# Attention heads: f32 products of latents in three passes of rounded parts

## The chip, the cores and the metric

The kernel runs on one core of a Trainium2 chip. The metric is the device time of one execution in microseconds (us).

## The reference

The kernel computes two blocks in f32. The first mixes 512 tokens of 1024 channels with a gated spatial layer and a recurrence. The second has latent attention with 16 heads, then a state space mixer. The change lies in the attention, which is this:

```python
def block(args):
    qa, qr, cs, sn = args
    q_pos = jnp.concatenate([qa, _apply_rope(qr, cs[:, None], sn[:, None])], axis=-1)
    q_free = jnp.concatenate([qa, qr], axis=-1)
    s_all = jnp.concatenate([jnp.einsum('bthd,bkd->bhtk', q_pos, keys_lat),
                             jnp.einsum('bthd,bkd->bhtk', q_free, keys_ctx)], axis=-1)
    p = jax.nn.softmax(s_all.astype(jnp.float32) * scale, axis=-1).astype(ckv_l.dtype)
    return (jnp.einsum('bhtk,bkc->bthc', p[..., :s], ckv_l)
            + jnp.einsum('bhtk,bkc->bthc', p[..., s:], ckv_c))
```

`keys_lat` and `keys_ctx` are the 128 latent channels `ckv` with 64 rope channels `kr` behind them, for 512 tokens and for 256 tokens of context. The context's queries attend to the context alone.

## The kernel before

Each engine runs its own program in order, and semaphores (`at(step)`) join them. TensorE (PE) is written out by hand in `head_pe`, ScalarE (ACT) in `head_act`, VectorE (DVE) in `head_dve`. SyncE (SP) loads the weights in the order of one stream, each tile of 512 KB into one of 6 ring slots when the tile 6 places ahead of it has been used.

**Input projection** (`mla_in_pe`, `mla_in_act`, `mla_in_dve`): 20 weight tiles, each 8 steps of a 256- and a 512-column product in f32. ACT evacuates each tile. PE sums the latents' squares beside it and transposes the normalized latents behind tile 15; DVE copies them to `ckv_tm` (L2257). In between DVE makes 16 tiles of powers for the state space mixer (`c_pow_dve`, L2043 and L2045, 6 operations each), which GpSimd stores: tiles 0 to 5 first, 12 to 15 behind `ckv_tm`. GpSimd makes tables (`tables_pool`) once all 16 are stored.

**Heads** (`head_pe`): a head has six units n of 128 queries: two of the context with 256 keys, four with 768 keys. For each unit:
- *scores*: the queries `q_abs` by the latents `ckv` (L2306), then the rope part (L2317), into one of two pairs of PSUM banks; always two units together;
- *softmax*: DVE takes the maximum (L2426, L2428), ACT the exp (L2446), DVE normalizes (L2435, L2437);
- *transposes* (`turn`, L2331): 2 or 6 into PSUM banks 6 and 7, and ACT copies them to SBUF (`pt_act`, L2456 or L2461). The banks are there once, so the next unit's transposes wait for that copy.

For each head come the *values* (L2342, 2 context tiles and 6 latent tiles of 512 columns), their copy `o_lat` (L2515), the up-projection (L2349) and the gate product on DVE (L2533). The next head is prepared in three steps: *fold* (L2374), *abs* (L2378, makes `q_abs`, copied at L2474), *rope* (L2387, copied at L2477, turned on DVE at L2523 to L2528). PE's order in head h, with n its first unit: transposes n-2, scores n and n+1, fold h+1, transposes n-1, scores n+2 and n+3, values h-1, transposes n and n+1, scores n+4 and n+5 with the up-projection of h-1 inside, transposes n+2, abs h+1, transposes n+3, rope h+1.

An f32 matmul stands in the trace as two instructions, a matmul on values rounded to `fp32r` as one. The trace calls both f32. Other products of the kernel are already in three passes of rounded parts: x = high + low, and high x high + high x low + low x high is summed in PSUM (L470 and L2739, for instance).

**Output projection** (`mla_out_pe`, L2563): 8 tiles in f32; DVE adds the residual from `xT` and `ctxT` and makes 15 tiles of powers (`b_pow_dve`, L2170). It begins when all engines have ended the heads.

## Time and profile before

| what | us |
|---|---|
| median of 3 runs | 2201.29 |
| lowest, highest | 2197.02, 2205.79 |
| profiled execution, its time | 2202.79 |
| profiled execution, span | 2200.9 |
| PE busy | 2091.2 |
| DVE busy | 1241.8 |
| ACT busy | 768.8 |
| GpSimd busy | 626.4 |
| chain that ended last, share of PE | 88% |

The span is from the first to the last instruction. The time also has what lies around it. In the span the input projection runs from about 470 to 676 us, the heads from 676 to 1130 and the output projection from 1130 to 1296. Busy times of PE are modelled at the ends of matmuls, so starts are read from start to start.

### The profile page before, as it was taken

What the parts mean: (1) busy time and instruction counts of PE and PEld (TensorE: products, weight loads), DVE (VectorE), ACT (ScalarE), POOL (GpSimd) and SP (SyncE); (2) the same over time, 40 slices, a digit from 0 to 9 for tenths busy, and PEclk for the clock granted to TensorE, in tenths of its full rate; (3) what the DMA queues carried; (4) which work ended last, traced back from release to release, by engine and by line L of the source; (5) the groups of instructions that cost most, each with busy time, mean ns of one, the idle gap of its engine ahead of it and who ended that gap; (6) DMA issues with size and microseconds to landing.
All of it is one profiled execution on the core that took longest, in us unless ns stands there. A gap on an engine that the chain in (4) does not pass through costs nothing.

```text
span 2200.9 us, 38924 instructions
## 1 busy us (share of the span) xinstructions
PE 2091.2 (95%) x15596; PEld 1508.5 (69%) x15596; DVE 1241.8 (56%) x1897; ACT 768.8 (35%) x1425; POOL 626.4 (28%) x1129
## 2 busy tenths in 40 slices
PE   7999998999998999999989978999989999999996
PEld 6887787765554555555555647888867788888785
DVE  3367664459995444444448856888993233333344
ACT  3335543231103444444410026555544322232223
POOL 2543211410015888888811221111121000000000
PEclk9999999999999999999999999999999999999999
DMA  9221443422452111111126433999974222222221
GB/s 360 78 96 51 154 156 118 163 85 96 167 192 100 53 53 53 53 53 58 53 93 239 165 120 108 308 304 304 307 214 170 86 96 96 96 96 96 96 86 39
DMA packets 119411, 292.42 MB, mean 133 GB/s; under 512 B 11616, under 2 KB 57056, under 8 KB 113088
## 3 DMA queue, kind: packets, MB, share of 16 engines
q1 hardware_dynamic: 107072, 226.10, 30.9%
q0 software_dynamic: 12160, 63.84, 7.8%
q8 instruction: 124, 2.03, 0.4%
q14 instruction: 55, 0.45, 0.1%
HBM read 223.97 MB, written 65.93 MB: 132 GB/s over the span
## 4 chain that ended last, share of the span: by engine, by line
PE 88%; DVE 6%; ACT 2%; issue 2%; POOL 1%; DMA 0%; SPq 0%; DVEq 0%; ACTq 0%; POOLq 0%
PE psum L470 30%; PE psum L1867 8%; PE psum L2563 8%; PE psum L2739 6%; PE psum L2306 5%; PE psum L2342 5%; PE psum L2317 3%; PE psum L1142 3%; PE psum L2331 2%; PE psum L2387 2%; PE psum L2909 2%; PE psum L2378 2%; PE psum L304 2%; PE psum L2859 1%; PE psum L2968 1%
## 5 line engine op out<-in xcount | busy, mean ns | idle before, releaser
L470 PE MATMUL psum<-split,w_split 128*128 128x512 f32 x1632 | 371.5, 389 | 0.0
L470 PEld LDWEIGHTS psum<-split,w_split 128*128 128x128 f32 x1632 | 306.3, 188 | 63.8
L452 DVE TENSOR_TENSOR w_split<-ring,w_split 128x512 fp32r<-128x512 f32 x182 | 129.0, 709 | 308.7 <-ACT w_split L447 308.3
L2088 POOL TENSOR_TENSOR early<-early 128x8 f32<-128x8 f32 (+6 forms) x672 | 277.1, 412 | 52.8
L447 ACT ACTIVATE w_split<-ring 128x512 fp32r<-128x512 f32 x182 | 115.0, 632 | 335.3 <-PE psum L470 332.3
L1867 PE MATMUL psum<-early,ring 128*128 128x512 f32 (+1 forms) x544 | 176.3, 486 | 0.0
L2739 PE MATMUL psum<-h,u_w 128*128 128x256 f32 (+1 forms) x768 | 158.6, 352 | 14.8 <-ACT u_t L2651 11.4
L2563 PE MATMUL psum<-gate,ring 128*128 128x512 f32 (+1 forms) x512 | 165.4, 486 | 1.2 <-issue 1.2
L1867 PEld LDWEIGHTS psum<-early,ring 128*128 128x128 f32 x544 | 103.3, 190 | 71.2 <-issue 64.1
L2563 PEld LDWEIGHTS psum<-gate,ring 128*128 128x128 f32 x512 | 97.2, 190 | 69.3 <-issue 62.7
L2739 PEld LDWEIGHTS psum<-h,u_w 128*128 128x128 f32 x768 | 119.7, 193 | 34.6 <-issue 18.8
L470 PE MATMUL psum<-h,w_split 128*128 128x512 f32 x552 | 134.6, 404 | 7.9 <-DVE w_split L452 7.9
L470 PE MATMUL psum<-h_split,in_w 128*128 128x512 f32 x600 | 138.8, 391 | 0.5 <-POOL in_w L459 0.5
L459 POOL TENSOR_TENSOR u_w<-ring,u_w 128x512 fp32r<-128x512 f32 x42 | 54.0, 1285 | 276.1 <-ACT u_w L447 238.8
L470 PEld LDWEIGHTS psum<-h,w_split 128*128 128x128 f32 x552 | 106.3, 194 | 34.9 <-DVE w_split L452 5.4
L353 POOL TENSOR_TENSOR early<-xT 128x512 f32<-128x512 f32 x1 | 1.3, 1290 | 452.2 <-DVE xT L3287 452.2
L470 PEld LDWEIGHTS psum<-h_split,in_w 128*128 128x128 f32 x600 | 111.9, 188 | 25.9 <-ACT prev L806 0.8
L2306 PE MATMUL psum<-ckv,q_abs 128*128 128x256 f32 (+1 forms) x320 | 111.4, 480 | 8.2 <-ACT prob L2446 5.8
L2426 DVE TENSOR_REDUCE early<-psum 128x1 f32<-128x768 f32 (+1 forms) x96 | 74.9, 780 | 78.0 <-PE psum L2317 76.1
L2342 PE MATMUL psum<-area,ckv_tm 128*128 128x512 f32 (+1 forms) x256 | 102.5, 554 | 1.0 <-ACT area L2461 1.0
L459 POOL TENSOR_TENSOR in_w<-ring,in_w 128x512 fp32r<-128x512 f32 x50 | 77.3, 1545 | 78.0 <-ACT in_w L447 75.8
L2342 PEld LDWEIGHTS psum<-area,ckv_tm 128*128 128x128 f32 x256 | 48.4, 194 | 53.5 <-issue 50.3
(442 smaller groups left out, 3480.9 us busy)
## 6 DMA issues: line engine op xcount, KB each, us to landing
ring<-in_s_glu SPq DMA_DIRECT2D x64, 512.0 KB, 3.5
ring<-in_w_mod SPq DMA_DIRECT2D x48, 512.0 KB, 5.3
made_c_pow<-area POOLq DMA_DIRECT2D x16, 1152.0 KB, 4.8
c_pow<-made_c_pow SPq DMA_DIRECT2D x32, 576.0 KB, 5.2
ring<-in_s_in SPq DMA_DIRECT2D x32, 512.0 KB, 6.5
made_b_pow<-area POOLq DMA_DIRECT2D x15, 1024.0 KB, 4.5
b_pow<-made_b_pow SPq DMA_DIRECT2D x15, 1024.0 KB, 10.5
ring<-in_w_in SPq DMA_DIRECT2D x25, 512.0 KB, 3.5
```

Source lines behind the costliest of these rows:

```text
L447: nc.scalar.activation(rounded(buffer(u, 0)), source(u), ACT.Copy).then_inc(act_done, 1)
L452: nc.vector.tensor_tensor(rounded(buffer(u, 1)), source(u), buffer(u, 0), ALU.subtract).then_inc(dve_done, 1)
L459: nc.gpsimd.tensor_tensor(rounded(buffer(u, 1)), source(u), buffer(u, 0), ALU.subtract).then_inc(pool_done, 1)
L470: ins = nc.tensor.matmul(out, rounded(buffer(u, w)[:, ks]), values(x, k), start=(first and k == 0 and n == 0), stop=(last and k == UNIT_K ...
L1142: ins = nc.tensor.matmul(psum[half(odd), b, a + tt * CHUNK:a + (tt + 1) * CHUNK], lhs(half(odd), tt), rhs(half(odd), tt), start=True, stop ...
L1867: ins = nc.tensor.matmul(o, tile_w(("mla_in", m), k), h2[:, k, a:a + n], start=(k == 0), stop=(k == KD - 1))
L2088: nc.gpsimd.tensor_tensor(o, a, b, op).then_inc(pool_done, 1)
L2306: mm(o, q_abs_of(h, u), ckv[:, a:a + m], start=True, stop=False)
L2342: ins = mm(o, ckv_tm[:, k, :], pt[:, k, :], start=(k == 0), stop=(k == kt - 1))
L2426: v.tensor_reduce(sm[:, n % 3, 0:1], both(b)[:, 0:keys], AX.X, ALU.max).then_inc(dve_done, 1)
L2563: ins = nc.tensor.matmul(o, tile_w(("mla_out", 2 * m + k // KD), k % KD), gate2[:, k, a:a + n], start=(k == 0), stop=(k == KE - 1))
L2739: ins = nc.tensor.matmul(o, rounded(u_w[:, u % 4, w, kk * P:(kk + 1) * P]), h3_part(x, k)[:, a:a + size], start=(k == 0 and n == 0), stop= ...
```

## The change

The latent part of the scores and the latent part of the values go from f32 to three passes of rounded parts. The rope part, the context's values and all projections stay in f32.

- *Scores*: `q_abs` becomes `q_abs_high`, which ACT writes rounded in place of its plain copy, and `q_abs_low`, which DVE makes as PSUM minus high (two operations). `ckv` gets `ckv_high` (ACT, behind tile 14 of the input projection) and `ckv_low` (DVE).
- *Values*: for units 2 to 5 of a head ACT's copy of the transposes is rounded (`pt_high`), and DVE makes `pt_low_a` and `pt_low_b` as PSUM minus high (two operations a unit). `ckv_tm` gets `tm_high` (ACT, behind tile 18) and `tm_low` (DVE, right behind `ckv_tm`). The 6 transposes of a unit now lie in 768 adjacent columns, and fold uses the first 256 columns of bank 6.
- *Waits*: transposes wait for the low part of the unit before; rope waits for `q_abs_low`, fold for the low part of unit n-2, values for the last `pt_low`.
- *Memory*: `high` and `pt_low_a` lie where `xT` is, `pt_low_b` where `ctxT` is. So SP stores `xT` to HBM behind the first block (2 MB), and loads it and `ctxT` back (2 MB and 1 MB) when the last values are done. `mla_out_dve` waits for that.

```diff
+                if m == 14:
+                    act.wait_ge(x_kept, 16)
+                    act.wait_ge(*at("ckv_normed"))
+                    nc.scalar.activation(rounded(ckv_parts[0]), ckv[:, :], ACT.Copy).then_inc(act_done, 1)
+                    act.wait_ge(act_done, act_count.up("ckv_high"))
+                if m == 18:
+                    act.wait_ge(*at("ckv_tm"))
+                    nc.scalar.activation(rounded(high[:, 3, :]), ckv_tm[:, :, :].rearrange("p k c -> p (k c)"), ACT.Copy).then_inc(act_done, 1)
+                    act.wait_ge(act_done, act_count.up("tm_high"))
 
         def mla_in_dve(dve):
             v = nc.vector
...
+            dve.wait_ge(*at("tm_high"))
+            v.tensor_tensor(rounded(tm_low[:, :, :]), ckv_tm[:, :, :], tm_parts[0], ALU.subtract).then_inc(dve_done, 1)
+            dve.wait_ge(dve_done, dve_count.up("tm_low"))
+            v.tensor_tensor(rounded(ckv_parts[1][:, :]), ckv[:, :], ckv_parts[0], ALU.subtract).then_inc(dve_done, 1)
+            dve.wait_ge(dve_done, dve_count.up("ckv_low"))
             for m in range(12, KE):
                 c_pow_dve(dve, m)
...
                 pe.wait_ge(*at("q_abs", h))
+                pe.wait_ge(*at("q_abs_low", h))
+                if h == 0:
+                    pe.wait_ge(*at("ckv_low"))
...
-                        mm(o, q_abs_of(h, u), ckv[:, a:a + m], start=True, stop=False)
+                    for q_part, c_part in ((0, 0), (0, 1), (1, 0)):
+                        for o, a, m in keys(n):
+                            mm(o, q_abs_of(h, u, q_part), rounded(ckv_parts[c_part][:, a:a + m]),
+                               start=(q_part == 0 and c_part == 0), stop=False)
                 if between is not None:
                     up_values(between)
...
                     pe.wait_ge(*at("folded", n // UNITS + 1))
                 pe.wait_ge(*at("normed", n))
+                if n >= 1 and (n - 1) % UNITS >= 2:
+                    pe.wait_ge(*at("pt_low", n - 1))
                 for k in range(2 if u < 2 else 6):
-                    b = 6 + (u if u < 2 else k // 3)
-                    ins = nc.tensor.transpose(bank(b, (k % 3) * P, (k % 3 + 1) * P),
-                                              prob_of(n)[:, k * P:(k + 1) * P], mask("ident"))
+                    out = bank(6 + u, k * P, (k + 1) * P) if u < 2 else both(6)[:, k * P:(k + 1) * P]
+                    ins = nc.tensor.transpose(out, prob_of(n)[:, k * P:(k + 1) * P], mask("ident"))
                 ins.then_inc(pe_done, 1)
                 pe_count.up("turned", n)
 
...
                     pe.wait_ge(*at("q_pos", hh + 1))
-                for o, pt, kt in ((both(0)[:, 0:CTX], pt_ctx, 2), (bank(1), pt_lat, 6)):
-                    for k in range(kt):
-                        ins = mm(o, ckv_tm[:, k, :], pt[:, k, :], start=(k == 0), stop=(k == kt - 1))
+                pe.wait_ge(*at("pt_low", UNITS * hh + 5))
+                if hh == 0:
+                    pe.wait_ge(*at("tm_low"))
+                for k in range(2):
+                    mm(both(0)[:, 0:CTX], ckv_tm[:, k, :], pt_ctx[:, k, :], start=(k == 0), stop=(k == 1))
+                passes = ((0, 0), (0, 1), (1, 0))
+                for i, (tm, pt) in enumerate(passes):
+                    for k in range(6):
+                        ins = mm(bank(1), rounded(tm_parts[tm][:, k, :]), rounded(pt_part(pt, k)),
+                                 start=(i == 0 and k == 0), stop=(i == 2 and k == 5))
                 ins.then_inc(pe_done, 1)
...
                     if hh >= 2:
                         pe.wait_ge(*at("pt", UNITS * (hh - 1) - 2))
+                        pe.wait_ge(*at("pt_low", UNITS * (hh - 1) - 2))
                 if what == "abs":
...
+                    pe.wait_ge(*at("q_abs_low_ctx", hh))
                 if what == "fold":
                     for k in range(2):
-                        ins = mm(bank(6 + k, 3 * P, 4 * P), w[:, k * P:(k + 1) * P], w[:, 512:640], start=True, stop=True)
...
                         if part == 1:
                             pe.wait_ge(*at("q_abs", hh))
+                            pe.wait_ge(*at("q_abs_low", hh))
                         for k in range(2):
                             left = w[:, 256 + k * P + part * ROPE:256 + k * P + (part + 1) * ROPE]
                             for j in range(2):
...
             u = n % UNITS
             act.wait_ge(*at("turned", n))
+            if n == 0:
+                act.wait_ge(c_stored[0], 16 * KE // 2)
+                act.wait_ge(c_stored[1], 16 * KE // 2)
             if u == 0 and n > 0:
                 act.wait_ge(*at("values", n // UNITS - 1))
             if u < 2:
@@ -2457,9 +2518,8 @@
                                      bank(6 + u, 0, 2 * P).rearrange("p (k c) -> p k c", k=2), ACT.Copy).then_inc(act_done, 1)
                 act.wait_ge(act_done, act_count.up("pt", n))
             else:
-                dst = pt_lat[:, :, (u - 2) * P:(u - 1) * P].rearrange("p (b k) c -> p b k c", b=2)
-                nc.scalar.activation(dst, psum[:, 6:8, 0:3 * P].rearrange("p b (k c) -> p b k c", k=3),
-                                     ACT.Copy).then_inc(act_done, 1)
+                nc.scalar.activation(rounded(pt_high[:, :, (u - 2) * P:(u - 1) * P]),
+                                     both(6).rearrange("p (k c) -> p k c", k=6), ACT.Copy).then_inc(act_done, 1)
                 act.wait_ge(act_done, act_count.up("pt", n))
 
         def proj_act(act, what, h):
...
+                nc.scalar.activation(folded[:, :, :].rearrange("p k c -> p (k c)"), bank(6, 0, 2 * P), ACT.Copy).then_inc(act_done, 1)
                 act.wait_ge(act_done, act_count.up("folded", h))
             elif what == "abs":
                 for (o, a, n), what in zip(parts_of(0), ("q_abs_ctx", "q_abs")):
-                    nc.scalar.activation(q_abs[:, h % 2, a:a + n], o, ACT.Copy).then_inc(act_done, 1)
+                    if h == 0:
+                        act.wait_ge(*at("q_sq", 1))
+                    nc.scalar.activation(rounded(q_abs_high[:, h % 2, a:a + n]), o, ACT.Copy).then_inc(act_done, 1)
                     act.wait_ge(act_done, act_count.up(what, h))
             else:
                 nc.scalar.activation(q_raw[:, h % 2, 0:TILES], bank(0, 0, TILES), ACT.Copy).then_inc(act_done, 1)
...
+            def q_abs_low_of(hh):
+                for (o, a, n), high_part, what in zip(parts_of(0), ("q_abs_ctx", "q_abs"), ("q_abs_low_ctx", "q_abs_low")):
+                    dve.wait_ge(*at(high_part, hh))
+                    nc.vector.tensor_tensor(rounded(q_abs_low[:, hh % 2, a:a + n]), o, q_abs_high[:, hh % 2, a:a + n],
+                                            ALU.subtract).then_inc(dve_done, 1)
+                    dve.wait_ge(dve_done, dve_count.up(what, hh))
+
+            def pt_low_of(nn):
+                cols_of = slice((nn % UNITS - 2) * P, (nn % UNITS - 1) * P)
+                dve.wait_ge(*at("pt", nn))
+                next_head = (nn + 1) // UNITS + 1
+                if nn % UNITS == UNITS - 1 and next_head < HEADS:
+                    dve.wait_ge(*at("folded", next_head))
+                for low, ks in ((pt_low_a, slice(0, 2)), (pt_low_b, slice(2, 6))):
+                    src = both(6).rearrange("p (k c) -> p k c", k=6)[:, ks, :]
+                    nc.vector.tensor_tensor(rounded(low[:, :, cols_of]), src, pt_high[:, ks, cols_of],
+                                            ALU.subtract).then_inc(dve_done, 1)
+                    dve_count.up("pt_low", nn)
+
             if h < 0:
+                q_abs_low_of(0)
                 q_pos_of(0)
                 return
+            n = UNITS * h
+            if h > 0:
+                pt_low_of(n - 2)
             if h == HEADS:
+                pt_low_of(n - 1)
                 gated(h - 1)
                 return
-            n = UNITS * h
             for pair in range(3):
+                if pair == 1 and h > 0:
+                    pt_low_of(n - 1)
                 if pair == 2 and h > 0:
                     gated(h - 1)
                 softmax_dve(dve, n + 2 * pair)
                 softmax_dve(dve, n + 2 * pair + 1)
+                if pair == 2:
+                    pt_low_of(n + 2)
                 normalize_dve(dve, n + 2 * pair)
+                if pair == 2 and h + 1 < HEADS:
+                    q_abs_low_of(h + 1)
                 normalize_dve(dve, n + 2 * pair + 1)
+            pt_low_of(n + 3)
...
             h3_gain_dve(dve)
+            dve.wait_ge(x_back, 2 * 16)
             for m in range(KD):
                 b_pow_dve(dve, 2 * m)
...
                     sp.dma_start(lam, io["lam"]).then_inc(lam_loaded, 16)
+                if n == slot_of[("mla_in", RING)]:
+                    sp.wait_ge(*at("ln1", "out", KD - 1))
+                    sp.wait_ge(*at("h2", KD - 1))
+                    sp.dma_start(io["x_kept"], xT[:, :, :]).then_inc(x_kept, 16)
+                if n == slot_of[("head", HEADS - 1)] + RING:
+                    sp.wait_ge(*at("values", HEADS - 1))
+                    sp.dma_start(xT[:, :, :], io["x_kept"]).then_inc(x_back, 16)
+                    sp.dma_start(ctxT[:, :, :], io["ctxT"]).then_inc(x_back, 16)
                 if n == slot_of[("mla_out", 8)]:
                     for who in ("pe", "act", "dve", "pool"):
```

The order on DVE at the end of the input projection, before (L2257 is the copy to `ckv_tm`, L2043 and L2045 are `c_pow` tiles, L2523 is the rope of head 0):

```order
L2045 SCALAR_TENSOR_TENSOR area<-area,dve_tmp 128x1152 [waits dve_done]
L2257 COPY ckv_tm<-psum 128x768 [waits pe_done,dve_done]
L2043 TENSOR_TENSOR dve_tmp<-q_pos,power 128x1152 [waits c_stored_0,c_loaded_0,dve_done]
...
L2045 SCALAR_TENSOR_TENSOR area<-area,dve_tmp 128x1152 [waits dve_done]
L2523 TENSOR_TENSOR early<-psum,const 128x256 [waits pe_done,dve_done]
L2526 TENSOR_TENSOR q_pos<-early,const 128x256 [waits act_done]
L2528 TENSOR_TENSOR early<-early,q_pos 128x256 [waits dve_done]
```

and after, where the same operations are L2293, L2070, L2072 and L2585:

```order
L2072 SCALAR_TENSOR_TENSOR area<-area,dve_tmp 128x1152 [waits dve_done]
L2293 COPY ckv_tm<-psum 128x768 [waits pe_done,dve_done]
L2298 TENSOR_TENSOR tm_low<-ckv_tm,high 128x768 [waits act_done,dve_done]
L2300 TENSOR_TENSOR ckv_low<-ckv,high 128x768 [waits dve_done]
L2070 TENSOR_TENSOR dve_tmp<-q_pos,power 128x1152 [waits c_stored_0,c_loaded_0,dve_done]
...
L2072 SCALAR_TENSOR_TENSOR area<-area,dve_tmp 128x1152 [waits dve_done]
L2601 TENSOR_TENSOR q_abs_low<-psum,high 128x256 [waits act_done,dve_done]
L2601 TENSOR_TENSOR q_abs_low<-psum,high 128x512 [waits act_done,dve_done]
L2585 TENSOR_TENSOR early<-psum,const 128x256 [waits pe_done,dve_done]
```

Two subtractions have come ahead of the tiles 12 to 15, the first with a wait for ACT, and the low part of head 0's queries (L2601) stands behind them.

The order on DVE in a head from the third pair's last maximum on, before (L2437 normalizes, L2523 to L2528 is the rope of the next head, then the next head's first maximum):

```order
L2428 TENSOR_SCALAR early<-early 128x1 [waits dve_done]
L2435 RECIPROCAL early<-early 128x1 [waits act_done,dve_done]
L2437 TENSOR_SCALAR area<-area,early 128x768 [waits dve_done]
L2435 RECIPROCAL early<-early 128x1 [waits act_done,dve_done]
L2437 TENSOR_SCALAR dve_tmp<-dve_tmp,early 128x768 [waits dve_done]
L2523 TENSOR_TENSOR early<-psum,const 128x256 [waits pe_done,dve_done]
L2526 TENSOR_TENSOR q_pos<-early,const 128x256 [waits act_done]
L2528 TENSOR_TENSOR early<-early,q_pos 128x256 [waits dve_done]
L2426 TENSOR_REDUCE early<-psum 128x1 [waits pe_done,dve_done]
```

and after, where these are L2484, L2486, L2493, L2495 and L2585; L2613 are the low parts of the transposes:

```order
L2486 TENSOR_SCALAR early<-early 128x1 [waits dve_done]
L2613 TENSOR_TENSOR pt_low_a<-psum,pt_high 128x2x128 [waits act_done,dve_done]
L2613 TENSOR_TENSOR pt_low_b<-psum,pt_high 128x4x128
L2493 RECIPROCAL early<-early 128x1 [waits act_done]
L2495 TENSOR_SCALAR area<-area,early 128x768 [waits dve_done]
L2601 TENSOR_TENSOR q_abs_low<-psum,high 128x256 [waits act_done,dve_done]
L2601 TENSOR_TENSOR q_abs_low<-psum,high 128x512 [waits act_done,dve_done]
...
L2613 TENSOR_TENSOR pt_low_a<-psum,pt_high 128x2x128 [waits act_done,dve_done]
...
L2613 TENSOR_TENSOR pt_low_a<-psum,pt_high 128x2x128 [waits act_done,dve_done]
L2613 TENSOR_TENSOR pt_low_b<-psum,pt_high 128x4x128
L2484 TENSOR_REDUCE early<-psum 128x1 [waits pe_done]
```

The low parts stand between the maximum and the normalization, between the two normalizations, and ahead of the next head's first maximum.

The order on PE from the transposes of unit n+3 to the fold, before (L2331 transposes, L2387 rope, L2306 scores, L2317 their rope part, L2374 fold):

```order
L2387 MATMUL psum<-qn,ring 64x384 [waits act_done]
...
L2387 MATMUL psum<-qn,ring 64x384 [waits act_done]
...
L2331 MATMUL psum<-const,area 128x128 [waits dve_done,act_done]
...
L2306 MATMUL psum<-ckv,q_abs 128x256 [waits act_done] x2
L2317 MATMUL psum<-kr,early 128x256 [waits act_done]
...
L2374 MATMUL psum<-ring 128x128 [waits act_done,slot_loaded_1]
...
L2331 MATMUL psum<-const,dve_tmp 128x128 [waits dve_done,act_done]
```

and after, where these are L2380, L2445, L2352, L2364 and L2431:

```order
L2380 MATMUL psum<-const,prob 128x128 [waits dve_done,act_done]
...
L2445 MATMUL psum<-qn,ring 64x384 [waits dve_done,act_done]
...
L2445 MATMUL psum<-qn,ring 64x384 [waits dve_done,act_done]
...
L2380 MATMUL psum<-const,area 128x128 [waits dve_done,act_done]
...
L2352 MATMUL psum<-high 128x256 [waits act_done,dve_done]
L2352 MATMUL psum<-ckv_low,high 128x256
L2352 MATMUL psum<-high,q_abs_low 128x256
...
L2364 MATMUL psum<-kr,early 128x256 [waits act_done]
...
L2431 MATMUL psum<-ring 128x128 [waits dve_done,act_done,slot_loaded_1]
```

Rope, scores and fold have got waits for DVE, and a 256-column score product has become three.

## Rows read from the trace of the kernel before

**Rows 1.** Busy time by stage, heads 700 to 1113 us (columns: the line above it).
```profile
core 0: us, PE busy (x) PEld busy (x) DVE busy (x) ACT busy (x) POOL busy (x), PEclk, DMA share, GB/s
700.00:1113.00 413.00, 406.76 (x1756) 224.64 (x1752) 189.35 (x426) 179.13 (x349) 338.02 (x819) 1.00 0.15 56
```

**Rows 2.** Timeline of one head on PE: start us, us, engine, line, operation.
```profile
840.41 0.82 PE L2331 MATMUL psum<-const,prob 128*128 128x128 f32 x6
841.16 2.80 PE L2387 MATMUL psum<-qn,ring 128*64 128x384 f32 x16
843.89 0.87 PE L2331 MATMUL psum<-const,area 128*128 128x128 f32 x6
...
846.19 0.71 PE L2374 MATMUL psum<-ring 128*128 128x128 f32 x4
...
847.77 2.82 PE L2306 MATMUL psum<-ckv,q_abs 128*128 128x256 f32 x8 [0.21 <-ACT prob L2446]
...
852.01 6.28 PE L2342 MATMUL psum<-area,ckv_tm 128*128 128x256 f32 x16
858.13 0.38 PE L2331 MATMUL psum<-const,prob 128*128 128x128 f32 x2
```

**Rows 3.** The same head on ACT and DVE.
```profile
835.80 0.96 DVE L2533 TENSOR_TENSOR gate<-psum,gate 128x768 f32<-128x768 f32 x1 [1.88 <-PE psum L2349]
...
839.46 0.15 DVE L2428 TENSOR_SCALAR early<-early 128x1 f32<-128x1 f32 x1
...
842.74 0.81 ACT L2461 ACTIVATE area<-psum 128x768 f32<-128x768 f32 x1
...
844.08 0.42 DVE L2523 TENSOR_TENSOR early<-psum,const 128x256 f32<-128x256 f32 x1 [0.42 <-PE psum L2387]
...
844.86 0.81 ACT L2461 ACTIVATE area<-psum 128x768 f32<-128x768 f32 x1 [0.30 <-PE psum L2331]
...
859.81 0.19 ACT L2446 ACTIVATION_READ_ACCUMULATOR prob<-psum,early 128x1 f32 x1
...
863.01 0.96 DVE L2533 TENSOR_TENSOR gate<-psum,gate 128x768 f32<-128x768 f32 x1 [1.78 <-PE psum L2349]
```

**Rows 4.** Groups by line and form, whole span: busy, mean of one.
```profile
L470 PE MATMUL psum<-split,w_split 128*128 128x512 f32 x1632 | 371.5, 389 | 0.0
L470 PEld LDWEIGHTS psum<-split,w_split 128*128 128x128 f32 x1632 | 306.3, 188 | 63.8
...
L2437 DVE TENSOR_SCALAR dve_tmp<-dve_tmp,early 128x768 f32<-128x768 f32 x32 | 22.7, 708 | 1.1
```

**Rows 5.** Timeline of PE: f32 pairs of 512 and 256 columns, then pairs in rounded parts.
```profile
633.87 41.45 PE L1867 MATMUL psum<-early,ring 128*128 128x256 f32 x128
...
1516.88 2.36 PE L2739 MATMUL psum<-h,u_w 128*128 128x256 f32 x12
```

**Rows 6.** Timeline of DVE, ACT and PE before the heads.
```profile
639.83 0.96 DVE L2257 COPY ckv_tm<-psum 128x768 f32<-128x768 f32 x1
...
665.09 0.81 ACT L2212 ACTIVATE gate<-psum 128x768 f32<-128x768 f32 x1 [9.51 <-PE psum L1867]
...
672.85 1.36 DVE L2045 SCALAR_TENSOR_TENSOR area<-area,dve_tmp 128x1152 f32<-128x1152 f32 x1
...
680.96 2.80 PE L2387 MATMUL psum<-qn,ring 128*64 128x384 f32 x16 [0.53 <-ACT q_abs L2474]
```

**Rows 7.** Window after an idle stretch of PE, same columns as Rows 1.
```profile
1322.90:1327.00 4.10, 4.02 (x13) 3.48 (x14) 3.92 (x6) 3.65 (x5) 0.00 (x0) 0.50 0.00 0
```

**Rows 8.** Timeline at the end of the heads, PE and GpSimd.
```profile
1118.25 8.24 PE L2342 MATMUL psum<-area,ckv_tm 128*128 128x256 f32 x16 [0.96 <-ACT area L2461]
...
1130.22 0.53 POOL L2109 MEMSET early<- 128x512 f32 x1 [23.57 <-DVE gate L2533]
```

**Rows 9.** Timeline of DVE in the output projection.
```profile
1171.80 0.29 DVE L2579 TENSOR_SCALAR early<-ctxT 128x256 f32<-128x256 f32 x1 [3.48 <-PE psum L2563]
```

**Rows 10.** DMA issues from 1095 to 1320 us: KB each, us to landing.
```profile
ring<-in_mla_out SPq DMA_DIRECT2D x12, 512.0 KB, 4.3
```

37 lines of the change are left out of this document (32 added, 5 removed).

## The prediction

> **What bounds the kernel now.** I read the table by stage first. In the heads' stage TensorE (PE) is busy 406.8 of 413 us at a granted clock of 1.00, VectorE (DVE) 189 us and ScalarE (ACT) 179 us [rows 1]. So PE's own work sets the time there, and an edit on the other two costs nothing until PE has to wait for it. Then I read one head instruction by instruction on PE [rows 2] and the parts of ACT and DVE that PE waits for [rows 3]. A head comes back every 27.21 us (835.80 to 863.01 on DVE). PE's groups stand end to end in it; the one wait that is marked is 0.21 us at the scores' second pair (847.77). Last I read the entry into the stage [rows 6] and its end [rows 8], because a change on DVE shows where nothing covers it.
>
> **PE's passes: what they save.** In plain f32, 128 instructions take 41.45 us [rows 5] (four tiles, each 8 steps of a 256- and a 512-column product, each product two instructions): 32 pairs, 1.29 us for a pair, so 0.43 us for 256 columns and 0.86 us for 512. In rounded parts a 512-column pass takes 371.5/1632 = 0.228 us [rows 4]. Six pairs of 512 and 256 columns take 2.36 us [rows 5], of which the last matmul's own 0.39 us [rows 4] is pipeline; (2.36 - 0.39)/5.5 = 0.36 us for a pair, which leaves 0.13 us for 256 columns. Three passes: 0.39 us for 256 columns against 0.43, and 0.68 us for 512 against 0.86. A head has six 256-column and four 512-column score products and six 512-column value products: scores 6 x 0.04 + 4 x 0.18 = 0.96 us, values 6 x 0.18 = 1.08 us (of the 6.12 us from 852.01 to 858.13 [rows 2]). Together 2.0 us of 27.2; at a 256-column pass of 0.12 us it would be 2.2. I take **2.1 us a head**.
>
> Each of those passes has a weight load of its own, so the 0.36 us a pair shows that the loads are hidden. The Trainium skill (TensorE: Matmul & The Clock Gate, sections LDWEIGHTS and Back-to-back issue gap) says a load costs its columns over 1.2 in ns, that is 107 ns for 128, and that the spacing of a stream is set by load and matmul both; if they simply added, a 256-column pass would take an estimated 0.21 us, and the sum below would be some 23 us higher (18 such passes in each of 16 heads). The 0.36 us a pair speaks against it.
>
> **DVE's low parts: what they cost.** DVE gets for each of four units a head two subtractions from PSUM, 256 and 512 columns, and two more for the queries. A 768-column operation on PSUM and SBUF (the gate product) takes 0.96 us and a 256-column one 0.42 [rows 3], so 512 columns take 0.69 by the slope and a set of two 1.11, with the gap 1.15 us. Five sets are 5.7 us a head; DVE's 189 us in 413 leave room. But PE waits for each set, since the next transposes overwrite the PSUM banks it reads. I follow the head from the third pair's maxima on:
> - Unit n+2: DVE ends the second maximum at 839.61 [rows 3], the low part runs to 840.79, and the transposes of n+3 start at 840.85 instead of 840.41 [rows 2]: **0.45 us**.
> - Rope: its first half now waits for the low part of the queries' context columns. DVE has the normalization (0.71 us [rows 4] and its reciprocal) and then that 0.42 us, so until 842.1; PE, which would start at 841.6, waits **0.5 us**. Then low part, second normalization and the set of n+3, whose copy ends at 843.55 [rows 3]: about 845.0, when the shifted rope ends too, so under 0.1 us.
> - Unit n+4: its transposes start near 845.0. ACT's copy begins 0.97 us behind their start and takes 0.81 (843.89 [rows 2], 844.86 [rows 3]), DVE's set 1.15, each hand-over 0.06: PE may go on 3.05 us after the start. Ahead of the fold it has the transposes and the first scores with their rope part, 2.30 us before (843.89 to 846.19 [rows 2]) and 2.1 now. It waits **0.9 us**. The first maximum of the next head also comes behind this set, which leaves the 0.2 us wait at 847.77 as it is.
> - Unit n+5: its set is behind the folded copy, but the scores' second pair (4 us with the rope part) covers it. Nothing.
> - Third pair of scores: its second unit needs an exp that ends 1.87 us after the first transposes of the head (858.13 to 860.00 [rows 2, 3]). PE reaches it 0.24 us earlier than before and cannot use that: with the shift of the values it waits about **0.4 us**.
>
> Waits: 0.45 + 0.5 + 0.1 + 0.9 + 0.4 = 2.3 us against 2.1 saved. A head's period stays where it is, +0.1 us; over 16 heads **+2 us**. The bounds: a gain of 1.0 us a head if half the waits are covered after all, a loss of 0.7 if a set takes 1.3 us (between its 1.11 and the 1.38 of 0.96 + 0.42) and each of the four waits grows with it: -16 to +11 us.
>
> **The entry: what the moved wait costs.** This is the large term. The new low parts of the latents are put on DVE ahead of four of the c_pow tiles, and the first of them waits for ACT's rounded copy, which stands behind the evacuation of tile 18. Before, DVE copies ckv_tm at 639.83, and the four tiles run from 640.8 until 674.21 [rows 6], while PE is busy with tiles 16 to 19; DVE is then idle, and PE's rope product of head 0 starts at 680.96 [rows 6]. After, DVE stands from 640.8 until tile 18 has been evacuated (665.09 + 0.81) and rounded (0.85, an estimate from the 0.81 of the evacuation of the same size [rows 6]): 666.8. Then two subtractions of 0.96, and the four tiles, 674.21 - 640.79 = 33.4 us: until 702.2. Queued behind them is the queries' low part of head 0, 0.42 us, and now PE's rope waits for it: it starts at 702.8 instead of 680.96, **+21.9 us**. Nothing covers it, since PE's queue has only the heads behind that instruction. The clock falls with it: where PE resumes after an idle stretch at 1322.9 the granted clock is 0.50, its level of 1.2 GHz, for 4.1 us of work [rows 7]; 4 us at 1.2 GHz instead of 2.4 cost **+2 us**. GpSimd's tables start behind the last c_pow store and are late by 28 us as well; before, GpSimd has been idle for 23.6 us when the next stage begins [rows 8], and with the stage itself 28 us late that stays so.
>
> **The end.** In the last head there is no product of a next head between the transposes, so PE waits for each copy of ACT (0.96 us at the values [rows 8]) and now for each set behind it: four times 1.17 us, less 0.7 us for shorter values (partly at the low clock): **+4 us**.
>
> **DMA.** 2 MB of xT are stored during the input projection and 3 MB (with ctx) come back at the end of the heads. SP waits ahead of the store for steps that PE's first tile needs as well, and has 30 us of loaded tiles in the ring. At the end a 0.5 MB tile lands 4.3 us after its issue [rows 10]; six of them bound the return at 26 us. DVE starts its b_pow up to 20 us late for that. PE needs the first residual only at its third tile, some 41 us in (two tiles of 20.6), and DVE gains 3.5 us a tile (its idle time at 1171.80 [rows 9]). So nothing, up to a return of 35 us.
>
> **Sum.** Profiled time 2202.79 (span 2200.9 and 1.9 around it): + 21.9 + 2 + 4 + 2 = 2232.7. The median shown is 1.5 below the profiled run: **2231 us**, 1.3% slower.
>
> **The rivals.**
> - **The low parts are hidden** (not slower). PE would keep its 2.1 us in each of 16 heads: 2231 - 2 - 34 = 2195 us. For it: DVE is 46% busy in the stage. Against: the waits come from the chain transposes, copy, set, not from load. The points that decide are a net gain of 1.1 us a head (then within 0.5% of before) and 2.4 (faster). A part of it, a gain of 1 to 2 us, gives 2197 to 2213.
> - **DVE's chain grows**: GpSimd's tables run beside it, and the normalization's mean of 0.71 us [rows 4] hides a spread. A period of 28 us or more gives 2242 to 2260.
> - **The entry's wait does not reach PE** (the change does not do what its order says): only tail and heads stay, 2201.3 + 6 = 2207. Against: DVE takes its queue in order and 33.4 us of tiles stand behind the wait.
> - **Weight loads show.** At a bound of 0.19 us for every 256-column pass (the duration of one load [rows 4]): 18 x 0.06 us a head, 17 us in all, 2248.
> - **Both entry and low parts hidden**: 2201.3 + 4 - 34 = 2171.
>
> **How the numbers follow.** 0.68 for the forecast (2213 to 2242), 0.12 for a head gaining 1 us or more, 0.11 for the grown chain, 0.04 for the entry off the path, 0.02 for the weight loads, 0.03 for both hidden. Within 0.5% of before (2190 to 2212, about what a measurement of this kernel can tell from no change) lie the entry rival and over half of the second: 0.11. Faster 0.03, slower 0.86. The range takes the forecast's case and a little of both neighbours: 2210 to 2246.
>
> **What would show it.** On PE an idle stretch of some 22 us before the first rope product of the heads, with the clock at 0.50 behind it; on DVE no work from 641 to 667. A period of DVE's gate product of 27.0 to 27.6 us, with waits on DVE's low part at the transposes of n+3, the rope and the fold, the longest at the fold. The values' 18 passes in 4.1 us. PE's last values 4 to 5 us later against the last head's start. I am wrong if the rope product starts before 695, or if the period is under 26.2 or over 28.

## The result and the profile after

The changed kernel takes 2225.23 us (median; 2223.84 to 2229.58), the kernel before 2203.54 us in the same rounds: ratio 1.0101, 95% interval 1.0078 to 1.0123, so 1.0% slower. The prediction said 2231 (2210 to 2246), slower. The profiled execution has a span of 2222.9 us against 2200.9.

First the entry into the heads, DVE and then PE of the kernel after (start, us, engine, line, operation, in brackets idle time and what ended it). These rows answer to [rows 6]:

```profile
635.81 0.96 DVE L2293 COPY ckv_tm<-psum 128x768 f32<-128x768 f32 x1
665.95 0.96 DVE L2298 TENSOR_TENSOR tm_low<-ckv_tm,high 128x768 fp32r<-128x768 f32 x1 [29.18 <-ACT high L2255]
666.94 0.96 DVE L2300 TENSOR_TENSOR ckv_low<-ckv,high 128x768 fp32r<-128x768 f32 x1
667.93 1.36 DVE L2070 TENSOR_TENSOR dve_tmp<-q_pos,power 128x1152 f32<-128x1152 f32 x1
...
701.35 1.15 DVE L2601 TENSOR_TENSOR q_abs_low<-psum,high 128x256 fp32r<-128x256 f32 x2
```

And PE in the same stretch:

```profile
675.40 0.68 PE L2431 MATMUL psum<-ring 128*128 128x128 f32 x4 [1.05 <-ACT gate L2239]
676.62 2.85 PE L2435 MATMUL psum<-qn,early 128*128 128x256 f32 x8 [0.53 <-ACT early L2530]
701.92 4.81 PE L2445 MATMUL psum<-qn,ring 128*64 128x384 f32 x16 [22.46 <-DVE q_abs_low L2601]
```

DVE stands for 29 us behind ACT's rounded copy, then works off the four c_pow tiles (667.93 to 701.3), and PE stands for 22.46 us until DVE has made the queries' low part. The table by stage shows the clock behind it (window, length, PE busy, granted clock, DMA share, GB/s):

```profile
682.00:706.00 24.00, 4.08 (x14) 0.50 0.41 153
706.00:712.00 6.00, 3.82 (x25) 1.00 0.13 48
```

Next, one head on PE in the kernel after, from the abs products of the next head to that head's third pair of scores (it answers to [rows 2]):

```profile
857.48 2.75 PE L2435 MATMUL psum<-qn,early 128*128 128x256 f32 x8
860.47 0.84 PE L2380 MATMUL psum<-const,prob 128*128 128x128 f32 x6 [0.24 <-DVE early L2493]
861.65 2.80 PE L2445 MATMUL psum<-qn,ring 128*64 128x384 f32 x16 [0.34 <-DVE q_abs_low L2601]
864.64 0.84 PE L2380 MATMUL psum<-const,area 128*128 128x128 f32 x6 [0.19 <-DVE pt_low_b L2613]
...
867.75 0.68 PE L2431 MATMUL psum<-ring 128*128 128x128 f32 x4 [0.92 <-DVE pt_low_b L2613]
868.26 0.82 PE L2380 MATMUL psum<-const,dve_tmp 128*128 128x128 f32 x6
868.91 0.59 PE L2352 MATMUL psum<-high 128*128 128x256 f32 x2
869.34 0.52 PE L2352 MATMUL psum<-ckv_low,high 128*128 128x256 f32 x2
869.69 0.51 PE L2352 MATMUL psum<-high,q_abs_low 128*128 128x256 f32 x2
...
873.45 1.75 PE L2396 MATMUL psum<-pt_high,high 128*128 128x512 f32 x6
...
877.81 0.38 PE L2380 MATMUL psum<-const,prob 128*128 128x128 f32 x2
...
879.74 0.61 PE L2352 MATMUL psum<-high 128*128 128x256 f32 x2 [0.28 <-ACT prob L2504]
```

In order after the abs products: transposes of n+3, rope, transposes of n+4, fold, the third pair of scores. And PE's waits of all heads from 749 to 1120 us (us in total, times, longest):

```profile
PE psum L2431 <- DVE pt_low_b L2613: 11.1, 13, 0.9
PE psum L2445 <- DVE q_abs_low L2601: 6.8, 14, 0.7
PE psum L2352 <- ACT prob L2504: 3.9, 14, 0.3
PE psum L2380 <- DVE early L2493: 3.5, 13, 0.6
```

The gate product of DVE came back every 27.21 us before; now its periods lie between 26.76 and 27.53 us, 27.05 in the mean (747.09 to 1125.82 in 14 heads). The last head is longer: three of its four transposes and the values wait 2.1 to 2.8 us each, the values for instance (against 0.96 at [rows 8]):

```profile
1141.10 2.04 PE L2392 MATMUL psum<-area,ckv_tm 128*128 128x256 f32 x4 [2.11 <-DVE pt_low_b L2613]
```

Profiles of one kernel shift by a few us outside this stage: the fold of head 0 starts between 674.4 and 681.4 us in the runs below, and from mla_out's last product to the end it is 901 to 906 us. I therefore give for each run, beside its ratio, the **stretch** from the fold of head 0 to mla_out's first product. Before: 1130.17 - 676.37 = 453.8 us; after: 1152.44 - 675.40 = 477.0 us.

### The profile page after: what moved, and what is told of

It is laid out like the page before. It is cut to its first block, busy times and chain, and to the rows that moved or that the text cites. A ratio compares the mean times of both kernels' runs of the same rounds, so it can differ in the third digit from the quotient of the medians.

```text
span 2222.9 us, 39692 instructions
## 1 busy us (share of the span) xinstructions
PE 2062.4 (93%) x15852; PEld 1542.2 (69%) x15852; DVE 1328.4 (60%) x2059; ACT 770.6 (35%) x1427; POOL 624.0 (28%) x1129
## 4 chain that ended last, share of the span: by engine, by line
PE 82%; DVE 11%; issue 3%; ACT 3%; POOL 1%; DMA 0%; SPq 0%; ACTq 0%; DVEq 0%; POOLq 0%
PE psum L476 29%; PE psum L1894 7%; PE psum L2655 7%; PE psum L2832 6%; PE psum L2396 3%; PE psum L1148 3%; PE psum L2352 3%; PE psum L2364 2%; PE psum L3002 2%; PE psum L2445 2%; PE psum L310 2%; DVE early L2484 1%; PE psum L2952 1%; PE psum L3061 1%; PE psum L353 1%
## 5 line engine op out<-in xcount | busy, mean ns | idle before, releaser
L2832 PE MATMUL psum<-h,u_w 128*128 128x256 f32 (+1 forms) x768 | 157.6, 350 | 14.7 <-ACT u_t L2744 11.4
L359 POOL TENSOR_TENSOR early<-xT 128x512 f32<-128x512 f32 x1 | 1.3, 1291 | 452.3 <-DVE xT L3380 452.3
L2484 DVE TENSOR_REDUCE early<-psum 128x1 f32<-128x768 f32 (+1 forms) x96 | 74.7, 779 | 29.3 <-PE psum L2364 27.5
L2521 ACT ACTIVATE pt_high<-psum 128x768 fp32r<-128x768 f32 x64 | 52.0, 812 | 74.9 <-PE psum L2380 73.9
L2445 PE MATMUL psum<-qn,ring 128*64 128x384 f32 x256 | 46.8, 508 | 29.6 <-DVE q_abs_low L2601 29.6
L1258 POOL TENSOR_TENSOR AL<-AT,const 128x256 f32<-128x256 f32 x40 | 34.8, 870 | 134.9 <-ACT AT L1228 93.4
```

The costliest lines, as they stand in the source:

```text
L2445: ins = mm(psum[64 * j:64 * j + 64, part, 0:TILES], left, token_half(qn[:, k, :], j), start=(k == 0), stop=(k == 1))
L2484: v.tensor_reduce(sm[:, n % 3, 0:1], both(b)[:, 0:keys], AX.X, ALU.max).then_inc(dve_done, 1)
L2832: ins = nc.tensor.matmul(o, rounded(u_w[:, u % 4, w, kk * P:(kk + 1) * P]), h3_part(x, k)[:, a:a + size], start=(k == 0 and n == 0), stop= ...
```

## The entry: two ways of taking the wait away

**Low parts behind the c_pow tiles.** The edit to the changed kernel:

```
-            dve.wait_ge(*at("ckv_high")) ... both subtractions ...
             for m in range(12, KE):
                 c_pow_dve(dve, m)
+            dve.wait_ge(*at("ckv_high")) ... both subtractions ...
```

> The changed kernel with one edit: the two subtractions of the latents' low parts stand on VectorE (DVE) behind the c_pow tiles 12 to 15 instead of ahead of them. Theory A (the prediction's): the wait for ScalarE's rounded copy at the entry is all that makes the change slow. TensorE's (PE's) rope product of head 0 goes back from 701.9 to about 681 us, the stretch at clock 0.50 behind it goes with it, the heads stay at a period of 27.05 us and the tail stays 4.3 us longer: 2225.2 - 21.9 + 1 = about 2204, within 2 us of before (2203.5). Rival B: part of the 22 us comes from elsewhere in the entry (later tables of GpSimd, the two subtractions themselves ahead of the first scores); then the rope or the first scores still start late by 5 us or more, and the time is 2209 or above.

Measured: 2200.44 us, ratio 0.9984 (0.9972 to 0.9996), stretch 452.3. The rope of head 0 is back:

```profile
680.82 2.80 PE L2445 MATMUL psum<-qn,ring 128*64 128x384 f32 x16 [1.14 <-ACT high L2536]
```

Theory A holds, and a little more came back than the entry's 21.9 + 2: the mean period fell from 27.05 to 26.86. That is not the entry itself, since in the next run the entry's wait is gone too and the mean period is 27.04; the run with late tables, below, shows what the periods follow.

**ACT's copies two tiles earlier.** DVE's order stays; `if m == 18` becomes `if m == 16` where ACT makes its rounded copies.

> The changed kernel, order on DVE as it is (low parts ahead of the four c_pow tiles), but ScalarE makes the rounded copies behind the evacuation of the input projection's tile 16 instead of 18. Theory A: what costs is the place of ScalarE's copy, since DVE stands only until it is there. Two tiles are some 21 us of PE, so DVE stands some 5 us instead of 26, its c_pow tiles end near 681, the rope product of head 0 starts 2 to 4 us later than before (683 to 685), and the time is 2205 to 2208. Rival B: DVE's order itself costs (its work in the entry is slowed or GpSimd's tables late): 2215 or more.

Measured: 2205.02 us, ratio 1.0001 (0.9988 to 1.0015), stretch 456.0. DVE stands 8.23 us instead of 29.18, and PE's rope waits 1.82 us. So most of the price was that of ACT's place in the queue: with DVE's order as it was, 20 of the 25 us that the first run won are won. The stretch is 3.7 us longer than the first run's, through the rope's wait and a mean period of 27.04.

## What the passes give and the low parts take, apart

All runs from here on but one (the one with late tables) have the entry's order of the first. **Scores alone** (values in f32 again, and no low parts of the weights and of `ckv_tm`):

```
-                passes = ((0, 0), (0, 1), (1, 0))
-                for i, (tm, pt) in enumerate(passes): ...
+                for k in range(6):
+                    ins = mm(bank(1), ckv_tm[:, k, :], pt_high[:, k, :], start=(k == 0), stop=(k == 5))
```

> With the entry's order of the first run, and only the scores' latent part in three rounded passes; the weighted values are plain f32 products again and DVE makes no low part of the weights. Theory A (the passes save, the sets on the path from copy to transposes take it back): a 256-column product goes from 0.43 to 0.35 us and a 512-column one from 0.86 to 0.68, 1.2 us a head; left of the waits is the one of the rope for the queries' low part, at most 0.4 us. Period 26.4 us (before 27.21), tail as before: 2203.5 - 1 - 13 = about 2190. Rival B (the passes themselves save little, or PE cannot use it since the exp holds the scores anyway): period 27.0 or more, 2199 to 2203.

Measured: 2200.71 us, ratio 0.9976 (0.9961 to 0.9990), stretch 449.5, every period but the last head's 26.88 or 26.89. That is 0.32 us a head less than before, not 0.8. The rope waits 0.50 us; the trace puts it down to ACT, but the rows of DVE and PE show who came last:

```profile
844.10 0.42 DVE L2591 TENSOR_TENSOR q_abs_low<-psum,high 128x256 fp32r<-128x256 f32 x1 [0.31 <-ACT high L2526]
```

PE:

```profile
844.67 2.80 PE L2435 MATMUL psum<-qn,ring 128*64 128x384 f32 x16 [0.50 <-ACT high L2526]
```

DVE is idle before its subtraction (0.31 us), so this wait is no load: it is one more hand-over behind ACT's copy. A further 0.27 us goes at the third pair, where PE comes to ACT's exp too early.

**Values alone** (scores in f32, no low part of the queries):

```
-                    for q_part, c_part in ((0, 0), (0, 1), (1, 0)): ...
+                    for o, a, m in keys(n):
+                        mm(o, q_abs[:, h % 2, u * P:(u + 1) * P], ckv[:, a:a + m], start=True, stop=False)
```

> With the entry's order of the first run, and only the weighted values in three rounded passes (with DVE's four sets of low parts a head); the scores' latent part is plain f32 and the queries have no low part. Theory A: the values save about 1.1 us a head, and the waits at the transposes of n+3 (0.24 us), n+4 (0.2 us) and, longest, at the fold remain; since the first scores now take longer (plain f32, 0.35 us more ahead of the fold) the wait at the fold falls from 0.85 to about 0.5. Period about 27.1 and the tail 4 us longer: 2203.5 - 1 - 2 + 4 = about 2205. Rival B (the waits are those of the queries' low part): period 26.3, 2193.

Measured: 2215.55 us, ratio 1.0046 (1.0026 to 1.0066), stretch 462.8, period 27.57. My expectation was 10 us too low. The values save 0.99 us (5.13 instead of 6.12), and 1.36 us of waits stand against it:

```profile
871.52 0.85 PE L2374 MATMUL psum<-const,prob 128*128 128x128 f32 x6 [0.24 <-DVE early L2487]
...
875.54 0.85 PE L2374 MATMUL psum<-const,area 128*128 128x128 f32 x6 [0.44 <-DVE pt_low_b L2608]
...
878.56 0.68 PE L2425 MATMUL psum<-ring 128*128 128x128 f32 x4 [0.68 <-DVE pt_low_b L2608]
```

Without the rope's wait PE only comes earlier to the transposes of n+4 and waits there. The waits of one chain replace each other: the first run's kernel, which has the queries' low part too, waits 0.24, 0.34, 0.03 and 0.84 us from the transposes of n+3 to the fold, 1.45 us in all against 1.36 here. So the queries' low part costs 0.5 us where it is alone and about 0.1 beside the sets.

**No low part of the weights after head 0, and then none of the queries either.** Two runs that leave these parts out:

```
             def pt_low_of(nn):
+                if nn >= UNITS:
+                    return
...
             def q_abs_low_of(hh):
+                if hh >= 2:
+                    return
```

The first of them has the first edit alone.

> Both products in three passes, entry's order of the first run, but DVE makes the low part of the weights in head 0 alone (this leaves out a part of the computation: later heads multiply a stale low part). It prices the sets: all passes are still on PE. Theory A (the waits come from the hand-over from ScalarE's copy to DVE's set to PE): against the scores-only run (period 26.89) the values save the 0.99 us that they save in the values-only run (5.13 instead of 6.12), and the waits at fold and transposes are gone: 25.9 us a head, tail no longer than before's: 2203.5 - 1 - 21 = about 2182. Rival B (the rounded passes make PE wait for something else, ScalarE's exp at the second or third pair): period 26.4 or more, 2190 or above.

> As the run without the weights' low parts, and the queries' low part is made for heads 0 and 1 alone as well (this leaves out a part of the computation: later heads use stale low parts). What is left is the PE saving with no new work on DVE. Theory A: the rope's wait of 0.50 us, which the scores-only run shows, goes: period 25.4 us, 2203.5 - 1 - 29 = about 2174. Rival B: the rope waits for ScalarE's own copy of the same columns, as soon as PE is early: period 25.7 or more, 2179 or above.

Measured: 2183.17 us, ratio 0.9911 (0.9890 to 0.9931), period 25.95, stretch 435.4; and 2184.40 us, ratio 0.9918 (0.9895 to 0.9942), period 25.37, stretch 435.1. This is the ledger of a head, typical periods: before 27.21; PE's saving alone 25.35 (-1.86, with the 0.27 us at exp in it); with the queries' low part 25.93 (+0.58); with the sets too 26.75 (+0.82). The sum, 1.40 us, is the price of the low parts; how it divides depends on the order in which they are added, as the run with the values alone shows.

The second run has a shorter period by 0.6 us and is no faster. Its PE waits ahead of mla_out, and the row of GpSimd (first), beside PE's, says for what: the store of GpSimd's last table.

```profile
1109.41 0.09 POOL L2132 MEMSET early<- 128x1 f32 x1 [10.23 <-DMA made_table<-early]
```

```profile
1109.71 2.90 PE L2659 MATMUL psum<-gate,ring 128*128 128x256 f32 x6 [8.61 <-issue]
```

GpSimd's cover of 23.6 us [rows 8] is also a floor: whoever shortens the heads by more waits for it. The store itself is slow here: GpSimd waits 10.2 us for it, against 3.1 in the kernel before. The return of x is issued in the same moment (1098.62 us, the store at 1098.60).

## Is it the grain of the waits, or DVE's queue?

**Finer waits** on the first run's kernel:

```
                 for k in range(2 if u < 2 else 6):
+                    if k == 2 and after_low:
+                        pe.wait_ge(*at("pt_low", n - 1))
...
-                        pe.wait_ge(*at("pt_low", UNITS * (hh - 1) - 2))
+                        pe.wait_ge(*at("pt_low_a", UNITS * (hh - 1) - 2))
```

> The first run's kernel with the waits cut finer: transposes wait for the low part's half in bank 6 before their first two columns and for the half in bank 7 only before the third; the fold waits for the bank 6 half alone; on DVE the queries' low part goes ahead of the normalization of unit n+4, and the first maximum of a head goes between the two halves of the set of n+4. Nothing is left out. Theory A (the order of DVE's queue and the grain of the waits cost, not DVE's load): 0.2 us at the rope and 0.35 us from the fold to the second pair of scores: period 26.2 instead of 26.75, 2200.4 - 8 = about 2192. Rival B (PE is already at ScalarE's exp there, so that a wait for exp takes over each one removed): period 26.7, 2200.

Measured: 2201.17 us, ratio 0.9986 (0.9974 to 0.9998), stretch 452.2, period 26.94. My theory A fell: the period rose by 0.08 us in the mean. Two single heads compared, of 26.89 us here and 26.75 in the first run, show where it went. From the first abs product to the rope 0.34 us were won and from scores to fold 0.6, and 0.32 went back at the transposes of n+4, 0.31 between them and the scores, 0.44 behind the fold, where the second half of each set comes late. DVE works almost without a pause from the fifth maximum to the set of n+3 (first run's kernel, 861.21 to 868.6 us, with one pause of 0.23), so this order of its queue changed who waits and not the sum. Other orders were not tried.

**GpSimd beside it.** The changed kernel, with GpSimd held ahead of its seventh table until the gate product of head 9:

```
+                if m == 6:
+                    pool.wait_ge(*at("gated", 9))
                 b_bar_pool(pool, m)
```

> The changed kernel itself (low parts ahead of c_pow), with one edit: GpSimd waits ahead of its seventh table until the gate product of head 9, so that heads 5 to 9 run without GpSimd. The total says nothing, since the tables are some 110 us late for the next stage; the periods do. In the changed kernel they go up and down from 26.76 to 27.53 us. Theory A (GpSimd's tables lengthen DVE's normalization from 0.62 to up to 1.0 us, and since DVE is on PE's path the period follows): in the heads without GpSimd every normalization takes 0.62 and every period is 26.75, with at most head 6's or 7's longer for another reason. Rival B (the scatter comes from DMA or from PE): the periods of heads 5 to 9 scatter as before, 26.76 to 27.53.

Measured (2326.09 us, one execution): periods 27.35, 27.26, 27.14, 26.90, 27.13, then without GpSimd 26.76, 27.08, 26.77, 26.77. In those four all sixteen normalizations take 0.62 us; in the first two heads the first two behind the gate product take 0.85 to 1.03. Theory A holds, with one period (27.08) that has another reason. There DVE starts the first maximum behind the gate product 0.36 us late, though PE's scores and ACT's busy time are as in the other heads:

```profile
913.61 0.96 DVE L2486 TENSOR_REDUCE early<-psum 128x1 f32<-128x768 f32 x1 [0.88 <-PE psum L2366]
```

In every other head this idle time is 0.52 or 0.53 us. The same head has the same 0.36 us in the changed kernel and in the first two runs of this document; what causes it stays open.

GpSimd lengthens DVE's operations in SBUF, but not every one counts. When GpSimd is back, in the heads of 26.81, 26.78, 26.77 and 26.76 us, normalizations of up to 1.07 us occur and the period stays, because they are those of n+2 and n+3. The period follows the two behind the gate product, those of n+4 and n+5, ahead of the rope and the fold: together they take 1.24 to 1.33 us in the heads of 26.75 and 1.8 to 2.0 in those of 27.1 to 27.35. Their mean, without the odd head, is 1.57 us in the changed kernel, 1.58 with ACT's copies two tiles earlier and 1.37 in the first run, in the same order as the mean periods (27.05, 27.04, 26.86). Before, they varied too (mean 1.33) and the period stood at 27.21.

## Low parts beside PE

**Queries' low part from SBUF**, scores alone:

```
-                    nc.scalar.activation(rounded(q_abs_high[...]), o, ACT.Copy)
+                    nc.scalar.activation(q_abs[...], o, ACT.Copy)
...
+                nc.vector.tensor_copy(rounded(q_abs_high[:, hh % 2, :]), q_abs[:, hh % 2, :])
+                nc.vector.tensor_tensor(rounded(q_abs_low[...]), q_abs[...], q_abs_high[...], ALU.subtract)
```

> The scores-only run with one edit: ScalarE copies the latent queries from PSUM in plain f32, as in the kernel before, and DVE makes rounded and low part from that copy in SBUF (a copy and a subtraction of 768 columns). PE's rope then waits for ScalarE's copy alone. Nothing is left out. Theory A (a low part costs PE time only because it holds the PSUM bank that PE writes next): the rope's wait of 0.50 us goes, the period is 26.4 us instead of 26.89, and the stretch from the fold of head 0 to mla_out's first product is 449.5 - 8 = 441.5 us; ratio to before about 0.994. Rival B (DVE's added load, some 1.6 us a head instead of 1.15, delays maxima or normalizations that PE waits for): period 26.7 or more, and a wait on DVE's max or normalization instead.

Measured: 2193.44 us, ratio 0.9952 (0.9935 to 0.9969), period 26.37, with DVE busy 14.7 us a head instead of 13.5. The rope waits for nothing. More work on DVE, less time: the held bank was the price. The stretch is 449.1 and not 441.5, because PE stands 10.16 us ahead of mla_out for GpSimd's last table:

```profile
1125.32 1.19 PE L2645 MATMUL psum<-gate,ring 128*128 128x256 f32 x2 [10.16 <-issue]
```

Its store is issued at 1114.7 us, against 1108.0 in the scores-only run, and GpSimd waits 9.8 us for it. The lateness is a price of the edit: GpSimd's tables follow each other every 26.99 us in the mean instead of 26.50, and when the heads are over (last tables of the run with late tables) every 24.7 to 25.2. So DVE and GpSimd slow each other, and work in SBUF that takes PE's wait away moves the floor up.

**The same for the weights' sets**, both products in passes:

```
-                    nc.vector.tensor_tensor(rounded(low[...]), src, pt_high[...], ALU.subtract)
+                    nc.vector.tensor_copy(rounded(pt_high[:, ks, cols_of]), plain[:, :, cols_of])
...
+                    nc.vector.tensor_tensor(rounded(low[:, :, cols_of]), plain[:, :, cols_of], pt_high[...], ALU.subtract)
```

> Scores and values both in three passes, entry's order of the first run, and all low parts made beside PE: ScalarE copies transposed weights and queries from PSUM in plain f32, DVE makes rounded and low parts from SBUF, placed where its queue has room (sets of n+4 and n+5 behind the next head's first two maxima, of n+2 and n+3 behind the normalizations of n+4 and n+5), and the values take their passes in the order high, low of the latents, low of the weights. Nothing is left out. Theory A (what costs is the held bank, not DVE's load): no PE wait on a low part, period 25.4 (the run without low parts) to 25.9, tail 1 to 2 us longer than in the kernel before; the heads end some 20 us earlier than before, which is where GpSimd's tables end (PE waited 8.6 us for them in the run without low parts), so 2182 to 2186, ratio 0.991. Rival B (four sets of 1.9 us on DVE, lengthened by GpSimd, delay the maxima): period 26.5 or more, 2195 or above. Rival C: DVE's work in SBUF slows GpSimd's tables, PE waits for their end at mla_out more than 5 us though the heads are later than in the run without low parts.

Measured: 2226.83 us, ratio 1.0103 (1.0088 to 1.0117), period 28.75: rival B. DVE is busy 22.8 us a head and has one pause (0.47 us) from 868.7 to 890 us. Scores wait 1.77 us for the queries' low part, which stands behind a set and ends at 877.9, and the next head's maxima stand behind another:

```profile
878.80 0.68 DVE L2610 CAST pt_high<-xT 128x256 fp32r<-128x256 f32 x1
...
880.34 0.88 DVE L2614 TENSOR_TENSOR pt_low_b<-ctxT,pt_high 128x512 fp32r<-128x512 f32 x1
881.14 0.41 DVE L2481 TENSOR_REDUCE early<-psum 128x1 f32<-128x256 f32 x1
```

The first maximum's scores ended at about 880.0. So moving a low part off the bank paid while DVE had room at that place of the head, and not beyond; with sets from PSUM DVE was busy 17.4 us a head. This run changes DVE's order and that of the passes as well, and DVE is still idle 5.9 us a head elsewhere; whether another order would have found room was not tried. GpSimd's tables take 29.0 us each here, against 26.31 in the first run, so what rival C describes is there too, though the longer heads cover it: PE has no wait for GpSimd.

**PE no longer waits for GpSimd** at the end of the heads, on the kernel before last (scores alone, queries' low part from SBUF):

```
-            phase_end(pe, pe_count, "heads")
+            phase_end(pe, pe_count, "heads", others=("act", "dve"))
```

> The previous scores-only kernel with the low part of the queries made beside PE, and one more edit: at the end of the heads PE waits for ScalarE and VectorE alone, no longer for GpSimd, whose tables PE does not read in mla_out (VectorE and ScalarE still wait for them). Nothing is left out. In the run before, PE stood 10.2 us ahead of mla_out's first product until GpSimd's last table had landed. Theory A: that wait was the whole of it; mla_out starts about 1 us after the last gate product, the time falls by 9 us to about 2184, ratio 0.991. Rival B: the wait moves, since VectorE and the return of x are as late as before and PE waits for the first residuals two tiles later: 2190 or above. Rival C: mla_out's weights land late beside the return of x (11.6 us for 512 KB there), and PE waits for its second or third tile: 2188 or above.

Measured: 2188.94 us, ratio 0.9929 (0.9914 to 0.9945), stretch 442.8. mla_out starts 1.17 us after the last product of the heads, and PE has no wait in its 165 us, so there is no sign of B or C. But the time is nearer to their bounds than to A's 2184, and the profile doesn't show A's gain either. GpSimd's last table was there early in this execution:

```profile
1119.01 0.09 POOL L2132 MEMSET early<- 128x1 f32 x1 [4.16 <-DMA made_table<-early]
```

Here the store was issued 0.75 us ahead of the return of x, not 2 us behind it, and GpSimd waited 4.2 us for it instead of 9.8. In the two runs with a long wait PE began 0.3 us after such a row; at that distance the old wait would have held mla_out to about 1119.3 us (an estimate), and it started at 1118.67. So in this profile the edit is worth some 0.6 us, and the rest of the 9 us is that the store fell ahead of the return. The medians fell by 4.5 us (2193.44 to 2188.94), about as much as the two intervals leave uncertain. What is shown is that PE no longer depends on the store; how much that gives in the mean is not. It is the fastest complete version here, 0.7% faster than the kernel before.

## The prediction, step by step

- **Entry, +21.9 us:** right. From fold to rope of head 0 it was 4.59 us and is 26.52: +21.93. The run with DVE's order turned round gives it back.
- **Clock, +2 us:** right by itself (16 rope instructions take 4.81 instead of 2.80 us), but one side of the account was left out. The kernel before had a slow stretch of its own in head 0 (granted clock 0.51 from 688.7 to 692.2 us), which is gone after the long one: eight score instructions took 4.51 us against 2.82 later. That is 1.7 us back. Fold to gate product of head 0 grew by 21.1 us (50.61 to 71.69), where the terms for entry and clock say 23.9. The rest is PE's saving in head 0: in the first run, which has the slow stretch at the same place, rope to gate product takes 44.51 us against 46.02.

The row of the kernel before, PE:

```profile
688.27 4.51 PE L2306 MATMUL psum<-ckv,q_abs 128*128 128x256 f32 x8 [2.18 <-ACT prob L2446]
```

- **PE's saving, 2.1 us a head:** 1.86 measured, net of a 0.27 us wait at exp that I had booked as a wait, so 2.1 as predicted. Its parts err both ways: the values save 0.99 for 1.08, which leaves 1.1 for the scores' 0.96. A pair of 512 and 256 columns comes every 0.35 us (predicted 0.36): 869.34 to 869.69 in the head shown above, where a group of two is such a pair. The Trainium skill (TensorE: Matmul & The Clock Gate, Back-to-back issue gap) says that the spacing is set by load and matmul both. That the two would simply add was the prediction's reading and not the page's, and these rows go against it: every pass has its load, and the pair comes as fast as predicted with the loads hidden.
- **Waits, 2.3 us a head:** too high. In a typical head of the first run they are 1.67 (0.58 + 0.82 + 0.27); the changed kernel's mean period of 27.05 makes them 1.9 to 2.0, of which 0.3 is the lengthened normalizations above and the odd head. Term by term: transposes of n+3 0.24 for 0.45, rope 0.34 or more for 0.5, n+4 up to 0.2 for 0.1, fold 0.84 to 0.92 for 0.9, third pair 0.28 for 0.4; and the 0.21 us at the second pair, which I left standing, is gone, since fold and transposes now come behind the wait for the set. A set takes 1.02 us and not 1.15: its second half starts 0.34 us behind the first, which takes 0.42, while DVE's gap was counted in full. So the heads gave 0.15 us each instead of taking 0.1. The set's rows, of the first run's kernel, DVE:

```profile
867.59 0.42 DVE L2613 TENSOR_TENSOR pt_low_a<-psum,pt_high 128x256 fp32r<-128x256 f32 x1
867.93 0.68 DVE L2613 TENSOR_TENSOR pt_low_b<-psum,pt_high 128x512 fp32r<-128x512 f32 x1
```

- **End, +4 us:** +4.3 (gate product of head 14 to mla_out 22.30 before, 26.62 after).
- **DMA, nothing:** right. DVE's b_pow waits 6.30 us for ctx, and PE has no wait in mla_out. The return took 11 us (1148.86 to 1159.82), far under the 26 that the prediction allowed for.
- **Sum:** +29.9 us predicted on the profile, +22.0 in the profiles: 1.0 less from earlier stages, 2.8 in head 0, 4.2 in the heads (-2.2 for +2) and 0.3 behind mla_out's start, but 0.3 more at the end. The forecast's mechanism was right; the terms that missed are the heads' waits, the clock's other side and the saving in head 0. That the time itself is only 5.8 us off is in part luck: beside the changed kernel the kernel before took 2203.54 us and not the 2201.29 from which the sum starts.
- **Rivals:** the loaded-DVE one (period over 28) did not come in the changed kernel, but it did in the run with all low parts from SBUF. That GpSimd lengthens DVE's work is real at a smaller size, 0.1 us a head in the mean of the first run and 0.26 in the changed kernel. "Low parts hidden" would have been 25.35 us a head; the price of the low parts, 1.4 us a head, is now measured.

## What to carry to other kernels

A subtraction that reads PSUM behind another engine's copy is a third hand-over before TensorE may write the bank again. Count it in the chain of the bank, not in the engine's load, and if the engine has room at that place take the low part from the SBUF copy. Before placing a wait in an in-order queue, look at what stands behind it: here 33 us of independent tiles stood behind a wait for a copy that another order gave for nothing. And a saving in one stage ends where the slowest helper of that stage ends (here GpSimd's tables): look for that floor, and for what your own edit does to it, before adding up gains per head.
